# The opening of a two-layer hybrid backbone: conditions turned alone, token tiles turned among the first modulation slices, and the first two features projected as a pair

## The reference, cut to what matters

```
mod   = silu(c) @ w_mod[0] + b_mod[0]          # and the same with c_ctx for the context tokens
sh1, sc1, g1, sh2, sc2, g2 = split(mod, 6)     # 1024 columns each
h     = rms_norm(x, norm1[0]) * (1 + sc1) + sh1
z     = h @ w_in[0]                            # retention, gated linear attention, two attentions, gates
```

## Time and profile before

| | us |
|---|---|
| median of three timed runs | 2708.28 (2707.35 to 2708.29) |
| profiled execution | 2701.96 |
| its span | 2700.1 |
| TensorE busy in the span | 2567.7 (95%) |
| VectorE, ScalarE, GpSimd busy | 1357.3, 760.2, 1473.3 |
| mean granted TensorE clock | 0.984 |

### The profile page before, as it was taken

How to read it: one execution, slowest core, us unless ns; L and a number is a source line. 1 busy time by engine, 2 the same in 40 slices (tenths; PEclk the granted TensorE clock), 3 DMA queues, 4 the chain that set the end, 5 groups by cost and what they waited for, 6 DMA issues and landing times.

```text
span 2700.1 us, 37847 instructions
## 1 busy us (share of the span) xinstructions
PE 2567.7 (95%) x15408; PEld 2124.9 (79%) x15408; DVE 1357.3 (50%) x1877; ACT 760.2 (28%) x1276; POOL 1473.3 (55%) x1375
## 2 busy tenths in 40 slices
PE   5999999999999999999999999998998998999999
PEld 2788888877777888888878888797777667888777
DVE  3622156543477867555574453326753677512231
ACT  4611333432255621111120123133431454211200
POOL 3443556522423636666669426546734346688886
PEclk9999999999999999999999999999999899999999
DMA  7422411312312833444433463212321137433322
GB/s 268 149 79 80 132 52 61 89 51 71 85 42 75 290 107 112 125 125 125 125 98 109 125 213 78 85 47 76 81 63 50 51 100 230 118 98 97 92 86 80
DMA packets 378210, 285.10 MB, mean 106 GB/s; under 512 B 10309, under 2 KB 338729, under 8 KB 377526
## 3 DMA queue, kind: packets, MB, share of 16 engines
q1 hardware_dynamic: 375744, 279.81, 34.7%
q10 hardware_dynamic: 1686, 2.78, 0.3%
q0 software_dynamic: 608, 0.09, 0.0%
HBM read 253.28 MB, written 29.36 MB: 105 GB/s over the span
## 4 chain that ended last, share of the span: by engine, by line
PE 80%; DVE 10%; ACT 3%; POOL 3%; issue 2%; DMA 1%; ACTq 0%; DVEq 0%; SPq 0%; POOLq 0%
PE ps L527 18%; PE ps L528 17%; PE ps L529 17%; PE ps L1186 3%; PE ps L730 3%; PE ps L571 2%; PE ps L572 2%; PE ps L573 2%; PE ps L814 2%; DVE ffl L2464 2%; PE ps L834 1%; PE ps L939 1%; POOL w_lo L1340 1%; PE ps L1135 1%; POOL w_hi L1337 1%
## 5 line engine op out<-in xcount | busy, mean ns | idle before, releaser
L1337 POOL TENSOR_TENSOR w_hi<-ring,tiny 128x512 fp32r<-128x512 f32 x480 | 533.7, 1112 | 1012.1 <-PE ps L529 605.8
L527 PE MATMUL ps<-hh,w_hi 128*128 128x512 f32 (+1 forms) x2320 | 845.0, 364 | 11.2 <-DVE hl L2022 8.9
L1340 POOL TENSOR_TENSOR w_lo<-ring,w_hi 128x512 fp32r<-128x512 f32 (+1 forms) x568 | 798.8, 1409 | 83.7 <-ACT w_hi L1543 46.0
L528 PE MATMUL ps<-hl,w_hi 128*128 128x512 f32 (+1 forms) x2320 | 821.6, 354 | 0.0
L529 PE MATMUL ps<-hh,w_lo 128*128 128x512 f32 (+1 forms) x2320 | 820.7, 354 | 0.0
L527 PEld LDWEIGHTS ps<-hh,w_hi 128*128 128x128 f32 x2320 | 443.4, 191 | 106.0 <-issue 27.8
L529 PEld LDWEIGHTS ps<-hh,w_lo 128*128 128x128 f32 x2320 | 443.0, 191 | 61.7
L528 PEld LDWEIGHTS ps<-hl,w_hi 128*128 128x128 f32 x2320 | 443.9, 191 | 56.9 <-issue 1.1
L1662 ACT ACTIVATE arena<-ps,tiny,vec 128x768 f32<-128x768 f32 (+1 forms) x120 | 108.6, 905 | 192.9 <-DVE tiny L2199 186.4
L1834 ACT ACTIVATE arena<-ps,vec 128x768 f32<-128x768 f32 (+1 forms) x44 | 39.0, 886 | 424.4 <-PE ps L529 424.4
L2473 DVE SCALAR_TENSOR_TENSOR arena<-ps,vec,arena 128x511 f32<-128x511 f32 x66 | 43.6, 661 | 219.5 <-ACT arena L1834 218.7
(11 more groups left out here) (271 smaller groups left out, 3817.7 us busy)
## 6 DMA issues: line engine op xcount, KB each, us to landing
ring<-in_w_in SPq DMA_DIRECT2D x118, 512.0 KB, 4.0
ring<-in_w_mod SPq DMA_DIRECT2D x96, 512.0 KB, 3.9
ring<-in_w_up SPq DMA_DIRECT2D x88, 512.0 KB, 4.2
ring<-in_w_down SPq DMA_DIRECT2D x48, 512.0 KB, 3.7
ring<-in_w_out SPq DMA_DIRECT2D x32, 512.0 KB, 3.8
logits<-arena SPq DMA_DIRECT2D x32, 384.0 KB, 2.3
arena<-logits SPq DMA_DIRECT2D x32, 384.0 KB, 4.4
ring<-in_w_down SPq DMA_DIRECT2D x24, 384.0 KB, 3.3
```

The costliest lines, as they stand in the source:

```text
L527: pe.matmul(acc, wh[:, offset + k], hi[:, n, x:y], start=n == 0, stop=False)
L528: pe.matmul(acc, wh[:, offset + k], lo[:, n, x:y], start=False, stop=False)
L1337: pool.tensor_tensor(wh[:, 0:count], w, one[:].unsqueeze(2).to_broadcast([P, count, P]), ALU.mult).then_inc(*up("w_lead", ("lead", key, j)))
L1340: pool.tensor_tensor(wl[:, 0:count], w, wh[:, 0:count].bitcast(F32), ALU.subtract).then_inc(*up("w_split", ("split", key, j)))
```

## The change

- **Conditions alone.** The rows are laid out anew, so that c and c_ctx are the first 16 rows of their block. Their two DMAs are the first on ScalarE's queue, TensorE turns them by themselves as soon as they and `ident` are there, and ScalarE takes the Silu before it squares the first token tile.
- **Constants moved.** Nine small DMAs (decays, lambdas, gate bias, norms, gate weights) go from ScalarE's queue to SyncE's, behind the first four modulation chunks. VectorE waits for them before it evicts the turned vectors. The mask is no longer loaded ahead of the slices but, with `dist` and `rope`, behind feature 2.
- **Groups in the order 0, 2, 1, 3**, with the chunk of feature 0 behind the first of them and that of feature 1 behind the second. The first half of the scale (tiles 0 to 3) needs only groups 0 and 2.
- **All eight scaled token tiles** are turned among the four chunks of group 2, two behind each chunk.
- **Features 0 and 1 as a pair.** Tile by tile, TensorE multiplies both features, with the chunks of groups 1 and 3 and the turns of x between the tiles. Tiles 4 to 7 wait for the second half of the scale.
- **x tiles 0 to 3** share one pair of banks and are evicted by VectorE.
- **Groups 4 and 5** move two slots back (`FIRST_SLOT`): group 4 behind features 2 and 3, group 5 behind the two token pairs. The turn of group 5 comes behind the last token pair.

The core of the diff:

```diff
+FIRST_SLOT = {"ret": 2, "gla": 0, "gqa": 0, "dif": 0}
...
+FIRST_GROUPS = (0, 2, 1, 3)
+OPENING = [("f", 0, "ret", 0), ("f", 0, "ret", 1)]
...
-        order += [("msl", l, g, kk) for g in range(4) for kk in range(4) if l == 0]
+        for i, g in enumerate(FIRST_GROUPS if l == 0 else ()):
+            order += [("msl", l, g, kk) for kk in range(4)] + OPENING[i:i + 1]
...
             pe.wait_ge(semaphore("ident_in"), 16)
-            pe.wait_ge(semaphore("rows_in"), 16 * N_ROWS)
-            vectors_turned(1)
-            vectors_turned(0)
+            pe.wait_ge(semaphore("c_in"), 32)
+            room(("vec", "c"), 4)
+            pe.transpose(psum(("vec", "c"))[:, 0:VB_CW], rows[0:VB_CW, 1], ident[0:VB_CW, 0:VB_CW]).then_inc(
+                *up("pe_full", ("full", ("vec", "c"))))
...
+                    g0, g1, g2, g3 = FIRST_GROUPS
+                    for kk in range(4):
+                        modulation_slices(("msl", l, g0, kk))
+                    pe.wait_ge(semaphore("rows_in"), 16 * N_ROWS)
+                    vectors_turned(1)
+                    vectors_turned(0)
+                    next_chunk(OPENING[0])
+                    for kk in range(4):
+                        modulation_slices(("msl", l, g1, kk))
+                        if kk == 0:
+                            modulation_turned(g0)
+                        turn_tokens("xn", 2 * kk)
+                        turn_tokens("xn", 2 * kk + 1)
+                    pe.wait_ge(semaphore("vectors_in"), 16 * (len(loads) - N_HW))
+                    vectors_turned(2)
+                    vectors_turned(3)
+                    next_chunk(OPENING[1])
+                    modulation_slices(("msl", l, g2, 0))
+                    modulation_turned(g1)
...
+                def opening_pair():
+
+                    behind_tile = {-1: [(g2, 1), (g2, 2)], 0: [(g2, 3)], 1: [(g3, 0), (g3, 1)], 2: [(g3, 2), (g3, 3)]}
+                    for n in range(-1, KT):
+                        if n >= 0:
+                            opening_tile(n)
+                        for g, kk in behind_tile.get(n, ()):
+                            modulation_slices(("msl", 0, g, kk))
+                        if n in (1, 3):
+                            modulation_turned((g2, g3)[n // 2])
+                        if n >= 0:
+                            turn_tokens("x", n)
...
+                    if l == 0 and b == "ret":
+                        turned(b, nf + nt // 2)
...
+                if n == RING:
+                    for dst, src in loads[4:9]:
+                        sp.dma_start(dst, src).then_inc(semaphore("consts"), 16)
...
+                    decays()
+                    act.wait_ge(*at(("free", ("vec", 0))))
+                    modulation_columns(FIRST_GROUPS[0])
+                    tokens_out("xn", xn, 0)
+                    modulation_bias(FIRST_GROUPS[0])
+                    tokens_out("xn", xn, 2)
+                    tokens_out("xn", xn, 4)
+                    modulation_columns(FIRST_GROUPS[1])
+                    tokens_out("xn", xn, 6)
+                    modulation_bias(FIRST_GROUPS[1])
+                    act.wait_ge(*at(("scale_set", 1, 0)))
+                    for k in range(KT // 2):
+                        act.wait_ge(*at(("free", ("xn", k))))
+                        lead_of(k)
...
                     for k in range(KT):
+                        if k % 4 == 0:
+                            first_scale(k // 4)
...
+                        for n in {2: (0,), 3: (1, 2), 4: (3,)}.get(k, ()):
+                            tokens_out("x", xT, n)
```

More of the change, by code:

```diff
@@ L149, in slices_behind @@
 def slices_behind(l, b, slot):
-    groups = columns_between(l)[b]
-    return [("msl", l, groups[slot // 2], 2 * (slot % 2) + n) for n in range(2)] if slot // 2 < len(groups) else []
+    groups, slot = columns_between(l)[b], slot - FIRST_SLOT[b]
+    return [("msl", l, groups[slot // 2], 2 * (slot % 2) + n) for n in range(2)] if 0 <= slot // 2 < len(groups) else []
 def next_modulation(l):
@@ L529, in product @@
                     mm = pe.matmul(acc, wl[:, offset + k], hi[:, n, x:y], start=False, stop=n == whole - 1)
-                    if each and key == ("f", 0, "ret", 0):
-                        turn_tokens("x", n)
                 return mm
@@ L985, in turn_tokens @@
             def turn_tokens(kind, k):
-                key, first = (kind, k), 4 + 2 * (k % 2)
+                key, first = (kind, k), 4 if kind == "x" and k < KT // 2 else 4 + 2 * (k % 2)
                 for s, n in room(key, first, first + 1):
@@ L998, in vectors_turned @@
             def vectors_turned(i):
[L999 removed]
+                for s, n in room(("vec", i), 1 if i in (1, 2) else 3):
                     pe.wait_ge(s, n)
@@ L1036, in banks, with opening_tile @@
                     return (0, 1) if turn[0] % 2 else (2, 3)
+                def opening_pair():
[9 more added lines that the diff above has]
+                            turn_tokens("x", n)
+                def opening_tile(n):
+                    j, k = n // (KT // 2), n % (KT // 2)
+                    if n == 0:
+                        for key in OPENING:
+                            for sem, c in room(key, *banks()):
+                                pe.wait_ge(sem, c)
+                    for key in OPENING:
+                        if k == 0:
+                            pe.wait_ge(*at(("split", key, j)))
+                        for x, y in segs(T):
+                            mm = product(psum(key)[:, x:y], key, j, hh, hl, x, y, count=1, first=n, offset=k,
+                                         each=lambda k: ("hl", l, 1, k))
+                        if k == KT // 2 - 1:
+                            mm.then_inc(*up("pe_half", ("half", key, j), *([("full", key)] if j else [])))
                 for b in ORDER:
@@ L1040, in _ @@
                     lag = 4 if b == "ret" else 2
-                    for j in range(nf + lag):
+                    if l == 0 and b == "ret":
+                        opening_pair()
+                    for j in range(1 if l == 0 and b == "ret" else 0, nf + lag):
                         slot = j if j < nf else nf + (j - nf) // 2 if j < nf + nt and (j - nf) % 2 == 0 else None
@@ L1049, in _ @@
                             n = feature_order(b)[j]
-                            projection(("f", l, b, n), hh, hl, W[l] if is_q(b, n) else T, banks(), each=each)
+                            if ("f", l, b, n) not in OPENING:
+                                projection(("f", l, b, n), hh, hl, W[l] if is_q(b, n) else T, banks(), each=each)
                             if b == "ret" and j == 0 and l > 0:
@@ L1258, in _ @@
                 l = key[1]
+                if n == RING:
+                    for dst, src in loads[4:9]:
+                        sp.dma_start(dst, src).then_inc(semaphore("consts"), 16)
+                    sp.wait_ge(*at(("cleared",)))
+                    for copy, d in itertools.product(range(2), range(2)):
+                        sp.dma_start(gate_up_of(copy, d), A["gla_gate_up"][0, d]).then_inc(semaphore("consts"), 16)
                 if n >= RING:
@@ L1769, in _ @@
                             query_squares(l, b, feature_order(b)[j])
+                    if l == 0 and b == "ret":
+                        modulation_bias(columns_between(l)[b][-1])
                     if b in ("gqa", "dif"):
@@ L2015, in norm, with first_scale @@
                 if l == 0 and which == 1:
-                    modulation_scale(1)
-                    for k in (KT - 2, KT - 1):
-                        dve.wait_ge(*at(("free", ("xn", k))))
+                    def first_scale(h):
+                        for g in FIRST_GROUPS[2 * h:2 * h + 2]:
+                            dve.wait_ge(*at(("free", ("mt", g))))
+                        ks = slice(4 * h, 4 * h + 4)
+                        nv = vec[:, 0, VA_N1 + 4 * h:VA_N1 + 4 * h + 4].unsqueeze(2).to_broadcast([P, 4, 2])
+                        step(dve.scalar_tensor_tensor(out=a1[:, 0, ks], in0=modv[:, KT + 4 * h:KT + 4 * h + 4], scalar=1.0, in1=nv,
+                                                      op0=ALU.add, op1=ALU.mult), "scale_set", ("scale_set", 1, h))
                     def rest_of(k):
```

101 lines of the change are left out of this document (43 added, 58 removed).

## The result

The kernel after takes 2712.69 us in the median of 15 runs (2706.34 to 2718.84); the kernel before, in 15 runs between them, 2707.35 (2697.76 to 2713.06). The ratio is 1.0022 with a 95% interval of 1.0014 to 1.0031: **slower, by 6.0 us (3.8 to 8.4)**. The forecast was 2714.4, by 6.1 us on the sum. The profiled execution took 2713.07 us, with a span of 2711.2, 11.1 longer than the profiled one of before.

The account below looks back on a forecast made before the run. TensorE is 95% busy, so the opening counts only through the first token pair's start, which the strips gate. Strips 0.9 us later plus slices moved back 5.2 gave 6.1 on the 2708.28 median: 2714.4 us, range 2701 to 2722.

Parts of the forecast that it names:

- Conditions, slices, root: Opening: zeroing of the Silu's operand at about 13 us, first slice at 18.5 or up to 3 sooner, root near 21.
- Constants: Small constants on SyncE's queue: ready for VectorE at 22.3 us, between 21 and 24, setting the scaling's start at 24.3.
- Scalings: Six token tile scalings on VectorE beside GpSimd's split of feature 0: 4.07 us plus 2.7, ending at 31.1.
- First tile of the pair: TensorE's first matmul of features 0 and 1 together: at 46.6 us, against 56.40 before; expected window 44 to 49.
- Wait in the middle: Before tile 4 of the feature pair, TensorE idles 3.3 us for bias and second half of the scale, to 67.6.
- Second half: Tiles 4 to 7 of the feature pair with their turns of x: 11.9 us, last turn ending at 79.5.
- rival 3: Slower still: constants at 24, scaling stretched by the whole split, lower clock again at tile 4; +5.6 us, 2720; chance 0.15.
- Strips to pair: From first strip exponential to first token pair: 28.6 us as before, so 85.6 to 114.2, 0.9 us later.
- over 8 was given as a sign: Sign of being right: over 8 us of TensorE waiting for ScalarE's feature eviction before the token pair near 114.
- with nothing of TensorE's in it: Claim about the kernel before: the 28.6 us from first strip exponential to first token matmul hold no TensorE work.
- rival 1: Faster: opening's waits absent and strips follow, token pair at 100.7, 12.6 us earlier; -7.4 us, 2700.9; chance 0.16.
- Slices moved back: Behind the token pairs, where TensorE has no hole: slices and turn 3.0 us, waits 1.4 and 0.8; together 5.2.

Follow-up runs that it names:

- e3: Kernel after with ScalarE's strip 0 behind feature 1's eviction, strip 1 behind feature 2's, strips 2 and 3 behind feature 3's; ratio to before 1.0019.
- e8: Kernel after with feature 2 in banks 4 and 5, feature 3 in 0 and 1, strip 0 behind feature 1, strips 1 to 3 behind feature 3; ratio 0.9983.
- e1: Kernel before with only modulation groups 4 and 5 moved two slots back; ratio to before 1.0025.
- e5: Kernel after with GpSimd's split of feature 0's first weights held until the six scalings are done; ratio to before 1.0023.
- e6: Kernel after with VectorE waiting for the small constants behind the six scalings and ScalarE's decays behind group 0's bias; ratio to before 1.0014.
- e12: Kernel before with only ScalarE's strip order changed: strip 0 behind feature 1's eviction, strips 1 to 3 behind feature 3's; ratio to before 0.9996.
- e7: Kernel after with the edits of e8, e6 and e2 together; 2695.36 us, ratio to before 0.9959.
- e9: Kernel after with groups 4 and 5 back in the old places, so the new opening alone; 2707.43 us, ratio to before 1.0011.
- e2: Kernel after with slices one slot back instead of two, last group's turn between the last token pair's halves, its bias ahead of the value evictions; ratio to before 1.0015.
- e4: Kernel after with feature 2 in banks 4 and 5 and feature 3 in banks 0 and 1; ratio to before 1.0050.

## Why the prediction was right

The two steps that carried the forecast are shown: the pair waits for evictions behind the strips, so the earlier features are not used (e3, e8), and the slices cost TensorE about 5 us where it has no hole (e1). Three things were off at the score, by 2.4, 0.4 and 2.9 us, all the same way. In order:

*Conditions, slices, root.* 12.58 (13), first slice at 15.53 (18.5 or up to 3 sooner), root at 20.3 (21). *Constants:* 23.63, inside 21 to 24, 1.3 late. *Scalings:* 7.40 us (6.8); e5 gives 4.07 with the split out of the way, so the price was 3.3 us, between the two ends as placed. The 2.7 taken for it does not follow from its row: there two instructions were stretched by 1.62 us (2.48 against 0.86), which is 3.2 for four. The Trainium skill (SBUF — State Buffer, "SBUF: two separate sides") gives the shared pair of ports to whichever engine starts first, for its whole instruction, and has the other fully blocked. Here the split took 5.8 us (24.71 to 30.5) beside the scalings and 4.7 by itself in e5, and the pair of jobs, 4.07 + 4.7 us of work, was done in 7.7 us from 24.71, where 8.8 would be one behind the other: delayed on both sides, but by less than the page's rule would make it.

*First tile of the pair:* 48.80 (46.6), inside the window. The 2.2 us are 0.7 of constants, 0.6 of scaling and 0.9 of the token turns and what follows them; e6's first tile is at 46.56. *Wait in the middle:* 2.86 us (3.3). *Second half:* from 69.74 to the last turn at 83.2, 13.5 us (11.9). **This is the mis-sized term of the opening**: tile 4 again ran at the lower level (0.77 us for its first matmul, 0.50 at tile 6, which starts at 77.40), which the forecast had kept for rival 3. With the 2.1 us late start (69.74 for 67.6) it put the last turn at 83.2 (79.5) and the first strip exponential at 89.28 (85.6), outside the window of 83 to 88.

*Strips to pair:* 27.3 us (28.6). So the pair at 116.56 is 3.3 late where 0.9 was forecast. The hole ahead of it was 6.89 us, where over 8 was given as a sign: feature 2 began at the lower clock level (0.63 us a matmul for 0.40) behind its own wait. That the strips carry this stretch was right for the kernel after (e3: 112.87 with them moved). As a reading of the kernel before it was half right: "with nothing of TensorE's in it" is refuted by e12, where TensorE alone gives the same 113.27 to 0.02 us. It did no harm, as the strips were the later of the two from then on. It does change what rival 1 could have been: an earlier strip chain would have given nothing without earlier features 2 and 3. e8 and e7 had both.

*Slices moved back:* 5.6 us (5.2), shown alone by e1 (5.6) and undone by e9 (0.6 left) and in part by e2 (2.3 left). *Not forecast:* the gate parts at the lower level behind the two short waits, 2.9 us (2.8 in e1). It stands in no term and no rival.

The sum at the score was therefore 11.8 us in the two profiles where 6.1 was forecast, and the timed ratio gives 6.0. The agreement to 0.1 us is partly luck: the stage itself lost nearly twice what was forecast, as much as rival 3's sum (11.7). Its three causes (constants, scaling, the clock at tile 4) each showed, two of them in small part: with 0.9 us of the turns they make 3.7 at the first strip exponential, and strips to pair took 1.3 less. Over the thirteen kernels the score's shift and the timed one go together (from -5.3 with -11 us to +13.5 with +13.5), but a single one scatters by several us about that, e5 (+10.9, 6.2 timed) and e2 (+12.4, 4.1 timed) as well as after. The drift of the traces is no sign that later stages give anything back: between 420 and 1080 us before's trace has 27.3 us at the lower clock level and after's 17.1, but e12's, whose score is within 0.7 us of before's, has 17.1 too, and its distance to before falls from +0.7 to -4.4 us by 1000 us. How much of after's other 5.8 us belongs to such draws of the clock, and how much to the quick profiled execution of before, was not settled.

Where did the gain go? A whole feature projection moved ahead of 83 us, and TensorE gave it back in two waits: 4.82 us ahead of 88.02, for the banks that feature 0 had to leave, and 6.89 ahead of 116.56, for an eviction that stood behind the strips in ScalarE's order.

## What to carry to other kernels

When work moves ahead of a chain, look at what the next consumer waits for in the order of the *other* engine: here the evictions stood behind decay strips that nobody needed yet. The new order of ScalarE and the other banks together turned 1.0022 into 0.9983, and with the later wait for the constants and the slices one slot back it was 0.9959. Before calling one chain the bound, remove it in thought and ask what arrives next: two chains may arrive within 0.03 us. And work moved out of a hole must find another: slices and a turn cost nothing next to a 3.4 us wait (e1's pair is no earlier without them), 5.6 us where there was none, and they made TensorE wait 6.1 us where they kept a ring of four from fetching.

## What the runs showed of the hardware

- VectorE and GpSimd hold each other up, tiny operations too: six scalings 4.07 us alone and 7.40 beside a split; a 128x16 operation 0.18 and 0.87 us; strip combinations 1.09 and up to 2.07.
- Two waits of 1.10 and 0.81 us with 1.05 us of work between them were followed by a mean granted clock of 0.75 over 12 us in after, and by 1.00 in e3 with the same two waits (1.09 and 0.81). The same instructions can meet either, and it is worth 2.9 us here.
- Moving a split moves the collision: from the scalings to the decays in e5 (3.3 us gone there, the first tile only 0.4 earlier), onto the strip combinations in e2, e4 and e9.
